# Sums of squares as two rounded products, and the ends of chunks in another order, in a hybrid recurrence kernel

## What is computed

```python
def head_rmsnorm(o, w):
    return o * lax.rsqrt(jnp.mean(o * o, axis=-1, keepdims=True) + NORM_EPS) * w.astype(jnp.float32)
def l2norm(x):
    return x * lax.rsqrt(jnp.sum(x * x, axis=-1, keepdims=True) + L2_EPS)
...
        o_b = from_chunks(hgrn2_chunked(qb, kb, vb, log_f))
        y_b = head_rmsnorm(o_b, hgrn_norm_w[l]).reshape(bsz, seq, -1) * jax.nn.silu(b_z.astype(f32))
...
        qc = jnp.repeat(l2norm(qc.reshape(bsz, seq, GDN_QK_HEADS, GDN_DK)), rep, axis=2) * GDN_DK ** -0.5
        kc = jnp.repeat(l2norm(kc.reshape(bsz, seq, GDN_QK_HEADS, GDN_DK)), rep, axis=2)
...
        y_c = head_rmsnorm(from_chunks(o_c), gdn_norm_w[l]).reshape(bsz, seq, -1) * jax.nn.silu(c_z.astype(f32))
```

## Time and profile before

| | |
|---|---|
| median of 3 runs | 2840.01 us (2838.42 to 2840.51) |
| profiled execution | 2846.03 us, span 2844.3 us |
| mean granted clock of PE | 0.982 |
| busy, share of the span | PE 96%, DVE 65%, POOL 52%, ACT 44% |
| the recurrence | about 1641 to 2291 us of the span |

### The profile page before, as it was taken

How to read it: one execution, slowest core, us unless ns; L and a number is a source line. 1 busy time by engine, 2 the same in 40 slices (tenths; PEclk the granted TensorE clock), 3 DMA queues, 4 the chain that set the end, 5 groups by cost and what they waited for, 6 DMA issues and landing times. The chain is left out here.

```text
span 2844.3 us, 39387 instructions
## 1 busy us (share of the span) xinstructions
PE 2730.9 (96%) x14135; PEld 2287.0 (80%) x14135; DVE 1849.3 (65%) x2902; ACT 1240.7 (44%) x2154; POOL 1472.0 (52%) x1135
## 2 busy tenths in 40 slices
PE   6899999999998999999999969999999989999999
PEld 5788888888886888888888858888888867887887
DVE  6677777772337788887723258887888865454453
ACT  6443434444444434344444335655556543222221
POOL 0555555554445555555544366667776534453541
PEclk9999999999999999999999969999999999999999
DMA  5333333333463333333334356654556557555552
GB/s 173 102 105 97 111 97 96 111 104 99 109 170 116 107 96 112 96 97 111 104 97 111 108 133 154 153 132 123 136 152 154 135 177 233 159 171 175 177 174 77
DMA packets 536937, 366.05 MB, mean 129 GB/s; under 512 B 65462, under 2 KB 469032, under 8 KB 536744
## 3 DMA queue, kind: packets, MB, share of 16 engines
q1 hardware_dynamic: 536744, 363.52, 44.9%
HBM read 251.27 MB, written 112.20 MB: 128 GB/s over the span
## 5 line engine op out<-in xcount | busy, mean ns | idle before, releaser
L765 POOL TENSOR_TENSOR w_low<-w_raw,w_high 128x512 fp32r<-128x512 f32 x480 | 684.7, 1432 | 637.5 <-ACT w_high L841 637.4
L795 PE MATMUL p_x<-h_high,w_high 128*128 128x512 f32 x1280 | 501.1, 392 | 16.9 <-POOL w_low L765 7.5
L795 PE MATMUL p_x<-h_high,w_low 128*128 128x512 f32 x1280 | 500.6, 391 | 0.0
L795 PE MATMUL p_x<-h_low,w_high 128*128 128x512 f32 x1280 | 500.3, 391 | 0.0
L841 ACT ACTIVATE w_high<-w_raw 128x512 fp32r<-128x512 f32 x480 | 296.8, 626 | 245.1 <-PE p_z L795 141.2
L795 PEld LDWEIGHTS p_x<-h_high,w_high 128*128 128x128 f32 x1280 | 241.7, 189 | 69.2 <-POOL w_low L765 7.6
L795 PEld LDWEIGHTS p_x<-h_low,w_high 128*128 128x128 f32 x1280 | 241.9, 189 | 50.5
L795 PEld LDWEIGHTS p_x<-h_high,w_low 128*128 128x128 f32 x1280 | 241.7, 189 | 50.1
L795 PE MATMUL p_z<-h_high,w_high 128*128 128x512 f32 x640 | 249.0, 389 | 0.0
L795 PE MATMUL p_z<-h_high,w_low 128*128 128x512 f32 x640 | 249.0, 389 | 0.0
L795 PE MATMUL p_z<-h_low,w_high 128*128 128x512 f32 x640 | 249.0, 389 | 0.0
(11 more groups left out here) (302 smaller groups left out, 6092.3 us busy)
## 6 DMA issues: line engine op xcount, KB each, us to landing
w_raw<-in_w_in_dram SPq DMA_DIRECT2D x160, 512.0 KB, 5.2
branch_scratch<-ring SPq DMA_DIRECT2D x176, 256.0 KB, 5.2
gate_scratch<-ring SPq DMA_DIRECT2D x96, 256.0 KB, 6.1
m_gt<-gate_scratch SPq DMA_DIRECT2D x96, 256.0 KB, 3.9
hin<-branch_scratch SPq DMA_DIRECT2D x16, 1280.0 KB, 11.6
zin<-branch_scratch SPq DMA_DIRECT2D x16, 1024.0 KB, 7.1
m_wo_raw_lead<-in_w_out_c_dram SPq DMA_DIRECT2D x43, 256.0 KB, 3.0
xin<-in_x_dram SPq DMA_DIRECT2D x16, 512.0 KB, 4.2
```

Of the source, the lines that this page charges most:

```text
L765: nc.gpsimd.tensor_tensor(wl[:, j, :, :], place(p, j), wh[:, j, :, :].bitcast(F32), ALU.subtract).then_inc(low, 1)
L795: x = nc.tensor.matmul(to[:], w[:, j, k, :], h[:, j, k, :], start=(opens and k == 0 and a == 0), stop=(k == HK - 1 and a == 2), skip_group ...
```

## The change

A sum of squares becomes two matmuls in F32R (a rounded f32 type) against `ones_r`: one over the rounded squares and one over what rounding left. So each square is needed as a rounded tile, as an exact one, and as their difference.

- Keys and queries: ACT squares them twice (`sq_high` rounded, `sq` exact), between `level_exp` 7 and `copy_e`; POOL's `squares` becomes the subtraction `sq_low`. The first chunk's stay as they were.
- The results: after `products_o` and `products_ho` ACT squares twice, to `sqc` and `qg`, and to `sqh` and `qe` (`qg` and `qe` are free by then). POOL subtracts in new steps `rest_c` 0, `rest_c` 1 and `rest_h`, at the end of its chunk. `weigh_c` and `weigh_h` on DVE wait for the second of the two squares (`sqc_exact`, `sqh_exact`); PE's norms wait for the rest.
- PE's order: `products_ho` goes ahead of `norm_c` 0, and `products_hds` ahead of `norm_c` 1. ACT's order of `rstd_c` 0, `square_h`, `rstd_c` 1 stays.
- `la_t`, `sq_high` and `sq_low` lie in the merge stage's tile `yl`; SP's `lead_in`, which fills that tile, waits for the last reads.

```diff
-        la_t = sb("la_t", [P, 2, V, P], F32R)
+        la_t = lead["yl"][:, 0:4, :].rearrange("p (i a) (b n) -> p i (a b) n", i=2, n=P)
+        sq_high, sq_low = lead["yl"][:, 4:6, :], lead["yl"][:, 6:8, :]
...
                 def load_k(w):
                     wait(sp, w - 1, "qkn_ready", 2)
-                    wait(sp, w - 1, "sq_ready", 1)
+                    if w > 1:
+                        sp.wait_ge(sems["sq_exact"], w - 1)
...
                 def lead_in():
+
+                    wait(sp, win - 1, "m_gb", 2)
+                    wait(sp, win - 1, "m_ssq", 2)
...
                 def squares(v):
-                    pool.wait_ge(k_in, 16 * v)
-                    wait(pool, v - 1, "m_ssq", 2)
-                    tt(sq[:].rearrange("p a (b n) -> p (a b) n", n=P), kin[:], kin[:], ALU.mult).then_inc(sems["sq_ready"], 1)
+
+                    pool.wait_ge(sems["sq_exact"], v)
+                    tt(flat(sq_low), flat(sq), flat(sq_high).bitcast(F32), ALU.subtract).then_inc(sems["sq_ready"], 1)
...
+                def rest_c(w, g):
+                    wait(pool, w, "sqc_exact", g + 1)
+                    tt(four(sqc_low, g), four(qg, g), four(sqc, g).bitcast(F32), ALU.subtract).then_inc(sems["sqc_ready"], 1)
+
+                def rest_h(w):
+                    wait(pool, w, "sqh_exact", 1)
+                    tt(flat(sqh_low), qe[:], flat(sqh).bitcast(F32), ALU.subtract).then_inc(sems["sqh_ready"], 1)
...
                     state_operands(w)
                     if v < win:
                         differences(v, 0)
+                    rest_c(w, 0)
+                    rest_c(w, 1)
+                    rest_h(w)
...
-                    mm(G[g][:], keep["ones"][:], four(sqc, g), start=True, stop=True).then_inc(sems["m_n"], 1)
+                    mm(G[g][:], ones_r[:], four(sqc, g), start=True, stop=False)
+                    mm(G[g][:], ones_r[:], four(sqc_low, g), start=False, stop=True).then_inc(sems["m_n"], 1)
...
                     products_ds(w, 0)
+                    products_ho(w)
                     norm_c(w, 0)
-                    products_ho(w)
+                    products_hds(w)
                     norm_c(w, 1)
-                    products_hds(w)
                     if v + 1 < win:
                         norms(v + 1)
                     norm_h(w)
...
+                def squares(v):
+                    act.wait_ge(k_in, 16 * v)
+                    wait(act, v - 1, "sq_ready", 1)
+                    wait(act, v - 1, "m_ssq", 2)
+                    keys = kin[:].rearrange("p a n -> p (a n)")
+                    fn(flat(sq_high), keys, ACT.Square)
+                    fn(flat(sq), keys, ACT.Square).then_inc(sems["sq_exact"], 1)
...
                 def square_c(w, g):
                     wait(act, w, "m_o", g + 1)
-                    fn(four(sqc, g), M[2 + g][:], ACT.Square).then_inc(sems["sqc_ready"], 1)
+                    fn(four(sqc, g), M[2 + g][:], ACT.Square)
+                    fn(four(qg, g), M[2 + g][:], ACT.Square).then_inc(sems["sqc_exact"], 1)
...
                 def square_h(w):
                     wait(act, w, "m_ho", 1)
-                    fn(sqh[:], HB[0][:], ACT.Square).then_inc(sems["sqh_ready"], 1)
+                    fn(sqh[:], HB[0][:], ACT.Square)
+                    fn(qe[:], HB[0][:].rearrange("p h n -> p (h n)"), ACT.Square).then_inc(sems["sqh_exact"], 1)
...
+                    if v + 1 < win:
+                        squares(v + 1)
                     copy_e(w)
...
-                    wait(dve, w, "sqh_ready", 1)
+                    wait(dve, w, "sqh_exact", 1)
                     stt(yh[:, u, :, :], HB[0][:], hw[:, 0:1], hin[:, u, ZH:ZH + H, :], ALU.mult, ALU.mult).then_inc(sems["t1h_ready"], 1)
```

More of the change, by code:

```diff
@@ L1303, in recur @@
         qg, ks, r, e = sb("qg", [P, V, P]), sb("ks", [P, V, P]), sb("r", [P, V, P]), sb("e", [P, V, P])
-        S, sqc = sb("S", [P, V, P]), sb("sqc", [P, V, P])
+        S, sqc, sqc_low = sb("S", [P, V, P]), sb("sqc", [P, V, P], F32R), sb("sqc_low", [P, V, P], F32R)
         yc, yh = sb("yc", [P, 2, V, P]), sb("yh", [P, 2, H, P])
@@ L1308, in recur @@
         egh, qe, ke, A = sb("egh", [P, H, P]), sb("qe", [P, HOP]), sb("ke", [P, H, P]), sb("A", [P, H, P])
-        vht, kht, sqh, SH = (sb(n, [P, H, P]) for n in ("vht", "kht", "sqh", "SH"))
+        vht, kht, SH = (sb(n, [P, H, P]) for n in ("vht", "kht", "SH"))
+        sqh, sqh_low = sb("sqh", [P, H, P], F32R), sb("sqh_low", [P, H, P], F32R)
         bank = lambda n: c.enter_context(nc.psum_tensor("b_" + n, [P, 4, P], F32))
@@ L1324, in recur @@
         count(rn_ready=4, dec_ready=2, eg_ready=2, vt_ready=2, kt_ready=1, hv_ready=1, w_ready=2 * levels,
-              h_exp=8, h_inv=1, e_h=1, e_ready=2, kht_ready=1, sqh_ready=1, sqc_ready=2, rnh_ready=2, rnc_ready=4, x_banked=1, x_ready=1, xt_ready=1)
-        count(sq_ready=1, la_ready=2, db_ready=1, dm_ready=1, dx_ready=8, qg_ready=1, ks_ready=1, qe_ready=1, ke_ready=1)
+              h_exp=8, h_inv=1, e_h=1, e_ready=2, kht_ready=1, sqh_exact=1, sqh_ready=1, sqc_exact=2, sqc_ready=2, rnh_ready=2, rnc_ready=4, x_banked=1, x_ready=1, xt_ready=1)
+        count(sq_exact=1, sq_ready=1, la_ready=2, db_ready=1, dm_ready=1, dx_ready=8, qg_ready=1, ks_ready=1, qe_ready=1, ke_ready=1)
         count(qkn_ready=2, ak_ready=2, aq_ready=2, x_set=1, x_step=steps, h_kq=8, h_pred=7, res=8, t_done=2, t_half=4, r_turned=6,
@@ L1478, in decayed_queries @@
                     wait(pool, w - 1, "m_o", 2)
+                    wait(pool, w - 1, "sqc_ready", 2)
                     tt(heads(qg), free_ap(qkn[:, 0, :], 0, [[P, Q], [0, 2], [1, P]]), heads(eg), ALU.mult).then_inc(sems["qg_ready"], 1)
@@ L1490, in state_operands @@
                     wait(pool, w - 1, "m_ho", 1)
+                    wait(pool, w - 1, "sqh_ready", 1)
                     tt(qe[:].rearrange("p (h n) -> p h n", n=P), hin[:, u, QH:QH + H, :], egh[:], ALU.mult).then_inc(sems["qe_ready"], 1)
@@ L1545, in norms @@
                     for g in range(2):
-                        mm(M[g][:], keep["ones"][:], sq[:, g, :], start=True, stop=True).then_inc(sems["m_ssq"], 1)
+                        if v == 0:
+                            mm(M[g][:], keep["ones"][:], sq[:, g, :], start=True, stop=True).then_inc(sems["m_ssq"], 1)
+                        else:
+                            mm(M[g][:], ones_r[:], sq_high[:, g, :], start=True, stop=False)
+                            mm(M[g][:], ones_r[:], sq_low[:, g, :], start=False, stop=True).then_inc(sems["m_ssq"], 1)
                 def sum_parts(bank, which, g):
@@ L1743, in norm_h @@
                     wait(pe, w, "sqh_ready", 1)
-                    mm(HB[1][:], keep["ones"][:], sqh[:], start=True, stop=True).then_inc(sems["m_hn"], 1)
+                    mm(HB[1][:], ones_r[:], sqh[:], start=True, stop=False)
+                    mm(HB[1][:], ones_r[:], sqh_low[:], start=False, stop=True).then_inc(sems["m_hn"], 1)
                 pe.wait_ge(zeroed, 2)
@@ L1930, in _ @@
                 level_exp(0, 0)
+                squares(1)
                 blocks_in(0)
@@ L2111, in weigh_c @@
                     for g in range(2):
-                        wait(dve, w, "sqc_ready", g + 1)
+                        wait(dve, w, "sqc_exact", g + 1)
                         stt(yc[:, u, 4 * g:4 * g + 4, :], M[2 + g][:], hw[:, 1:2], zin[:, u, V + 4 * g:V + 4 * g + 4, :], ALU.mult,
```

## The result

The changed kernel takes 2879.22 us (median of 4 executions, 2877.46 to 2885.35), the kernel before beside it 2840.26 us. The ratio is 1.013, with a 95% interval of 1.0107 to 1.0153: slower by 39 us. The forecast was 2869 us, with a range of 2850 to 2888. The profiled execution has a span of 2883.6 us, 39.3 us more than before; from the first chunk's end to the last one's (T of chunk 0 to T of chunk 15) it takes 603.5 us where it took 567.5, so 36.0 us of the difference lie there. Of the other 3.3 us, 0.2 lie ahead of chunk 0 (T at 1714.57 against 1714.35), where the forecast took nothing, and the rest behind T of chunk 15, 1.3 of it in that chunk's later norm_h.

The account below looks back on a forecast made before the run. The prediction took PE and the chain ACT to DVE to PE both to be at their limit in the chunk's end, with 0.13 us spare. 2840 + 15.7 (chain) + 13.6 (clock) = 2869 us, range 2850 to 2888.

Parts of the forecast that it names:

- T: In each chunk's end, the time when products_ds has ended; the forecast counts the later steps from it.
- the chain: Chunk's end, products_ho through ACT and DVE to state_h, then norm_h: turn_v 0.96 us later per chunk, 15.7 us in all.
- the falls: PE's granted clock drops behind the new wait before norm_h: 1.7 us each in 8 chunks, 13.6 us.
- the Squares of the keys: ACT's two Squares ahead of copy_e delay products_o by 0 to 0.1 us a chunk; taken as 0.
- The case that was given the largest chance: Chain longer with the clock falling in five or more chunks: 2862 to 2885 us, chance 0.47.
- The step that decides: On ACT, square_h stays behind rstd_c 0, which waits for the moved norm_c 0; Square starts at T+3.78.
- Half of the chunks: Clock falls in 8 of 16 chunks, since the 2.55 us wait lies between 2.10 (none) and 2.65 (fell).
- The one fall of today: Clock fall in the old recurrence without a long wait, mean 0.77 over 15 us; may stay or go, worth 3 us.
- Idle time before products_o ended by ACT's e: Sign of a wrong forecast, on PE: it would show that the keys' Squares cost time.
- The chunk of 38.1 us: Old chunk length, from norm products at 1865.78 and 1903.90; the forecast full-clock chunk after the change is 39.1 us.
- The pairs: On PE, two rounded products replace one f32 product: 0.51 us instead of 0.86, saving 0.35 us each.
- The rival that POOL and DVE get in each other's way: decayed_queries slows DVE's kql products 0.4 us a chunk: 2875 us, to 2888 with late copy_e and more falls; chance 0.07.

## Why the prediction was right, and where its sizes were off

The direction, the mechanism and the range were right; the median came out 10 us above the forecast. By the traces the terms are: the chain 14 us (forecast 15.7), the falls 22 less one that went, 18 us (13.6), the Squares of the keys 8 us (0). They add up to 40 us, and 39 were measured. The case that was given the largest chance, the chain longer and the clock falling in five or more chunks, is the one that came.

**The chain.** The forecast had norm_h at T+7.42 after 2.6 us of waiting and turn_v at T+7.93; measured are T+7.25 after 2.57 us and T+7.82. The growth at turn_v is 0.85 us, forecast 0.96: norm_c 0 started 0.07 us earlier than forecast, at T+1.71, and ACT's Ln 0.74 us behind it instead of 0.81. The step that decides, that square_h is held behind rstd_c 0, which waits for the moved norm_c 0, is shown twice: by the order alone (1.10 us a chunk, no doubled Square in it) and by the exchange of the two steps on ACT (norm_h back at T+6.13).

**The clock.** The price of a fall was right: 40.8 less 39.1 is 1.7 us. The number was mis-sized, 13 falls instead of 8, 22 us instead of 13.6. Half of the chunks was a guess between an idle time that cost the clock and one that didn't. The runs put more between them. Waits of 0.8 to 1.5 us before norm_h had no fall directly behind them in any of these chunks; those of 2.5 to 2.6 us had one in 12 and in 9 of 14 chunks, those of 3.0 to 3.1 us in 14 of 14. In the chunk without norms, waits of 2.11 and 2.30 us were followed by a fall once each, and waits of 2.30, 2.35 and 2.60 us were not. So between 2.1 and 2.6 us the length alone doesn't decide it, and what does stays open. The one fall of today (0.77 in the earlier trace rows) went, as was left open; that is 4 us in the other direction, and so it is partly luck that the forecast is off by no more than 10 us. It begins 22 us behind norm_h, and such a fall, without a long wait before it, also stands in the runs with the old order (20 us or more behind norm_h) and with state_h and the key norms earlier; its cause was not looked for.

**The Squares of the keys.** The step "Cost 0 to 0.1 us a chunk; I take 0" failed. PE is idle for 0.34 us before products_o, and moving the Squares gives 0.59 us a chunk, 8 us in all. The subtraction itself was off: two Squares of 1.9 to 2.0 us less 0.91 us of idle time make copy_e 1.0 to 1.1 us later and not 0.9 to 1.0, so that its first copy would end at 1897.3 to 1897.4, behind the 1897.25 at which products_o starts, and not at 1897.2 ahead of it. The Squares took 2.01 us from the first's start to copy_e's (2109.69 to 2111.70). Idle time before products_o ended by ACT's e was among the prediction's own signs of being wrong, and this one came.

**The base.** The chunk of 38.1 us in the prediction was not typical. The median was 37.7, and the agreement of the forecast of 39.1 for a full-clock chunk with the 39.1 measured is partly luck: 38.1 + 0.96 as against 37.7 + 0.85 + 0.5. Since the sum was made of differences, the error did not enter it.

**The pairs.** Forecast 0.51 us each, measured 0.47 (norms, 2083.52 to 2083.99 by their four matmuls), 0.54 (norm_c, 2081.64 to 2082.18) and 0.57 (norm_h).

**POOL.** Its three subtractions were hidden: rest_h ran from 2084.72 to 2085.99, ahead of norm_h's 2087.18. Two kql products of DVE that POOL's work covers took 1.07 and 1.09 us, where one had taken 0.69. This was hidden: PE has no wait for a kql product in this chunk. The rival that POOL and DVE get in each other's way thus cost nothing, although its first half came.

```profile
2088.97 1.07 DVE L2092 TENSOR_TENSOR kql<-hin,hx_inv 128x512 f32<-128x512 f32 x1 [1.24 <-ACT hx_inv L1876]
...
2089.96 1.09 DVE L2094 TENSOR_TENSOR kql<-hin,hx 128x512 f32<-128x512 f32 x1
```

The Trainium skill (SBUF — State Buffer, "SBUF: two separate sides") names such pairs, a VectorE instruction with two SBUF inputs and a GpSimd instruction that reads SBUF, as the ones that block each other. The two rows and that in the earlier trace rows agree: POOL's instruction that was under way (decayed_queries until 2089.49, then differences until 2090.51) ended 0.52 and 0.55 us after DVE's had started, and DVE's took 0.38 and 0.40 us more than the 0.69.

## What to carry to other kernels

An engine that is busy for 98% of a stage may have a second chain beside it with 0.1 us of room; before work is taken off the busy engine, measure the distance between its own arrival and that of the step that it would have to wait for. A step that is moved back on one engine moves every step that stands in line behind its reader on another: look at the reader's list, and move its neighbours with it. And price a new wait on PE twice, once for its length and once for the clock behind it.

## What was not expected of the hardware

More matmuls made the kernel faster: six useless ones per chunk in PE's wait of 2.6 us kept the granted clock at 1.00 in the first 14 chunks and took 14 us off the median (26 us between the profiled executions). Whether a given wait costs the clock is not a matter of its length alone: with the same 2.6 us, 12 of 14 chunks of one kernel and 9 of 14 of another had a fall, and in the first of them eight came in a row. One wait of 2.11 us was followed by a fall, and one of 2.60 us in another kernel was not.
